# RWKV-7 triangular inverse: first three merge levels on TensorE replaced by an 8x8 solve on VectorE, in another written order

## The reference, cut to what matters

```
def step(S, inp):
    r_t, w_t, k_t, v_t, kk_t, a_t = inp
    sa = -jnp.einsum('bhvk,bhk->bhv', S, kk_t)
    S = (S * w_t[:, :, None, :] + sa[..., None] * (kk_t * a_t)[:, :, None, :]
         + v_t[..., None] * k_t[:, :, None, :])
    return S, jnp.einsum('bhvk,bhk->bhv', S, r_t)
```

## Time and profile before

| | us |
|---|---|
| time, median of 3 runs | 1287.76 (1287.63 to 1289.8) |
| the profiled execution: its own time | 1285.7 |
| the profiled execution: span of the trace | 1283.9 |
| busy in the span: PE / PEld / DVE / ACT / POOL | 1249.1 / 1005.3 / 625.1 / 407.1 / 498.9 |
| mean granted TensorE clock | 0.98 of full speed |

### The profile page before, as it was taken

The page is one execution under the profiler, slowest core; times in us unless marked ns, Lnnn a source line. Parts: engine busy times, 40 slices in busy tenths (PEclk is TensorE's granted clock), DMA queues, the critical chain, the costliest instruction groups (busy, mean ns, idle before and its releaser), DMA issues.

```text
span 1283.9 us, 21631 instructions
## 1 busy us (share of the span) xinstructions
PE 1249.1 (97%) x8772; PEld 1005.3 (78%) x8772; DVE 625.1 (49%) x954; ACT 407.1 (32%) x598; POOL 498.9 (39%) x368
## 2 busy tenths in 40 slices
PE   7999999999999999999999999989999999999996
PEld 5877778888888888877867777767788888888885
DVE  4624666441114434447557767776554311344333
ACT  4644433221112222244443435324322211222110
POOL 0541445454445555533122011103555544455541
PEclk9999999999999999999899988979999999999998
DMA  7211212222222222221011000100222222222211
GB/s 272 100 66 66 99 66 99 98 99 99 98 97 74 93 99 95 98 99 66 3 67 35 35 34 2 68 2 35 99 99 98 98 99 98 99 98 98 99 66 65
DMA packets 17783, 105.17 MB, mean 82 GB/s; under 512 B 1968, under 2 KB 2480, under 8 KB 6064
## 3 DMA queue, kind: packets, MB, share of 16 engines
q1 hardware_dynamic: 17280, 103.75, 23.2%
q10 hardware_dynamic: 432, 0.38, 0.1%
HBM read 102.03 MB, written 2.10 MB: 81 GB/s over the span
## 4 chain that ended last, share of the span: by engine, by line
PE 90%; issue 3%; DVE 3%; POOL 2%; ACT 1%; DMA 0%; DVEq 0%; SPq 0%; POOLq 0%; ACTq 0%
PE ps L1015 61%; PE ps L1109 7%; PE ps L1166 3%; PE ps L1143 2%; POOL w_lo L583 2%; PE ps L1078 2%; PE ps L1419 2%; PE ps L1397 2%; PE ps L1435 1%; PE ps L1342 1%; PE ps L1278 1%; DVE cv L2054 1%; PE ps L1455 0%; PE ps L1463 0%; PE ps L1522 0%
## 5 line engine op out<-in xcount | busy, mean ns | idle before, releaser
L583 POOL TENSOR_TENSOR w_lo<-w_raw,w_hi 128x512 fp32r<-128x512 f32 x360 | 493.2, 1400 | 752.9 <-ACT w_hi L676 266.6
L1015 PE MATMUL ps<-h_hi,w_hi 128*128 128x512 f32 x688 | 277.2, 403 | 0.1
L1015 PE MATMUL ps<-h_lo,w_hi 128*128 128x512 f32 x688 | 269.6, 392 | 0.0
L1015 PE MATMUL ps<-h_hi,w_lo 128*128 128x512 f32 x688 | 269.5, 392 | 0.0
L1015 PEld LDWEIGHTS ps<-h_hi,w_hi 128*128 128x128 f32 x688 | 130.1, 189 | 35.2 <-issue 7.4
L676 ACT ACTIVATE w_hi<-w_raw 128x2048 fp32r<-128x2048 f32 x50 | 95.7, 1913 | 194.7 <-PE ps L1015 143.4
L1015 PEld LDWEIGHTS ps<-h_hi,w_lo 128*128 128x128 f32 x688 | 130.1, 189 | 27.8
L1015 PEld LDWEIGHTS ps<-h_lo,w_hi 128*128 128x128 f32 x688 | 130.4, 190 | 25.7 <-issue 0.5
L1015 PE MATMUL ps<-f_hi,w_hi 128*128 128x512 f32 x384 | 149.4, 389 | 0.0
L1015 PE MATMUL ps<-f_lo,w_hi 128*128 128x512 f32 x384 | 149.4, 389 | 0.0
L1015 PE MATMUL ps<-f_hi,w_lo 128*128 128x512 f32 x384 | 149.4, 389 | 0.0
(11 more groups left out here) (319 smaller groups left out, 1778.1 us busy)
## 6 DMA issues: line engine op xcount, KB each, us to landing
w_raw<-in_weights SPq DMA_DIRECT2D x91, 1024.0 KB, 4.9
x<-in_xT SPq DMA_DIRECT2D x8, 256.0 KB, 5.7
w_raw<-in_weights SPq DMA_DIRECT2D x8, 256.0 KB, 6.3
outT<-x SPq DMA_DIRECT2D x8, 256.0 KB, 2.0
masks_f<-in_masks SPq DMA_DIRECT2D x1, 512.5 KB, 6.2
sgu_ln<-in_sgu_ln SPq DMA_DIRECT2D x1, 512.0 KB, 8.2
low_w<-in_low_w SPq DMA_DIRECT2D x1, 512.0 KB, 7.2
sgu_w<-in_sgu_w SPq DMA_DIRECT2D x1, 256.0 KB, 6.7
```

What stands on the lines that cost most here:

```text
L583: piece = pool.tensor_tensor(w_lo[:, j, at], w_raw[:, j, at], w_hi[:, j, at].bitcast(f32), SUB)
L1015: mm = pe.matmul(bank(gb(g) if isinstance(i, int) else g % 2), w, r, start=(k == 0 and m == 0), stop=(k == K - 1 and m == 2))
```

## The change

Levels 0, 1 and 2 of the inverse leave TensorE. The diagonal 8x8 blocks (16 per matrix, 8 matrices) are inverted on VectorE by back substitution, and TensorE starts at level 3 (B = 8).

- `scores(c, 4)` on PE now makes L in 32x32 pieces (64x32 weights, twice as many matmuls as before); on DVE four masked copies gather the 8x8 blocks into `LT8` (128 partitions x 8 matrices x 8 columns).
- `solve(c, j)`, j = 6 down to 1, is new on DVE: a partition shuffle of 64 columns, a product with a broadcast column of `LT8`, and a sum, each waiting for the one before.
- `x_of(c)` is new on DVE: a masked copy of 512 columns spreads the solved blocks into `xtc`, and a 32x32 block transpose of 512 columns gives `xc`.
- ACT writes one identity per c and not two.
- The steps of levels 1 and 2 (`tx`, `dx`, `dxt`) are gone from all three lists, and the masks of the three levels with them; the lists stand in another order throughout: the same remaining steps, differently interleaved.

```diff
+BASE = 8
+FIRST_LEVEL = 3
+MERGES = LEVELS - FIRST_LEVEL
+X_STEPS = 4 + 3 * (BASE - 2) + 2
...
@@ scores(c, 4) on TensorE
-                        for to in COLUMN_HALVES:
-                            mm = pe.matmul(ps[to, 3 + h2, 32 * n:32 * n + 32], AR[r, c % 2, n, 0, to],
-                                           bT[r, n * P + to.start:n * P + to.stop:2], start=True, stop=True)
+                        for q in range(0, P, 32):
+                            mm = pe.matmul(ps[q:q + 32, 3 + h2, 32 * n:32 * n + 32],
+                                           bT[r, n * P + q:n * P + q + 32], AR[r, c % 2, n, 0, q:q + 32],
+                                           start=True, stop=True)
...
@@ tx on TensorE
-                if lv == 1:
-                    pe.wait_ge(s("x_init"), 4 * c + 2)
+                n = lv - FIRST_LEVEL
+                if n == 0:
+                    pe.wait_ge(s("x_step"), X_STEPS * (c + 1))
+                    pe.wait_ge(s("score_done"), 8 * c + 8)
                     pe.wait_ge(s("ktok1_done"), c + 1)
...
@@ on VectorE
+                for k in range(4):
+                    if c or k:
+                        dve.wait_ge(s("x_step"), X_STEPS * c + k)
+                    dve.copy_predicated(y4(LT8[:, :, :].rearrange("p y n -> p (y n)"), BASE), y4(mask(f"block{k}", 0, 8 * BASE), BASE),
+                                        ps[:, 3:5, 0:P].rearrange("p h (t n) -> p t h n", n=32)[:, :, :, BASE * k:BASE * k + BASE])\
+                       .then_inc(s("x_step"), 1)
+
+            def solve(c, j):
+
+                at = X_STEPS * c + 4 + 3 * (BASE - 2 - j)
+                z = LT8 if j == BASE - 2 else Z8
+                flat = lambda t: t[:, :, :].rearrange("p y n -> p (y n)")
+                dve.wait_ge(s("x_step"), at)
+                dve.stream_shuffle(flat(R8), flat(z), [BASE * (p // BASE) + j for p in range(32)]).then_inc(s("x_step"), 1)
+                dve.wait_ge(s("x_step"), at + 1)
+                tt(T8[:, :, :], R8[:, :, :], LT8[:, :, j:j + 1].broadcast_to([P, 8, BASE]), MUL).then_inc(s("x_step"), 1)
+                dve.wait_ge(s("x_step"), at + 2)
+                tt(flat(Z8), flat(z), flat(T8), ADD).then_inc(s("x_step"), 1)
+
+            def x_of(c):
+
+                at = X_STEPS * (c + 1) - 2
+                dve.wait_ge(s("x_step"), at)
+                dve.wait_ge(s("x_id"), c + 1)
+                dve.copy_predicated(xtc[:, :, :].rearrange("p y (b n) -> p y b n", n=BASE),
+                                    mask("blocks").rearrange("p (y b n) -> p y b n", b=8, n=BASE),
+                                    Z8[:, :, :].rearrange("p y (b n) -> p y b n", b=1).broadcast_to([P, 8, 8, BASE]))\
+                   .then_inc(s("x_step"), 1)
+                dve.wait_ge(s("x_step"), at + 1)
+                dve.transpose(xc[:, :, :].rearrange("p y n -> p (y n)"), xtc[:, :, :].rearrange("p y n -> p (y n)"))\
+                   .then_inc(s("x_step"), 1)
```

The parts of the written order on which most depends are those between `scores(c, 4)` and the first `tx` of c. On TensorE after the change, for c = 0, 1, 2, 3:

```diff
+            ("scores", 0, 4), ("slice", 7, 7), ("slice", 6, 0), ("zw", 1), ("tok_tr", 0, 0), ("tok_tr", 0, 1), *run("slice", 6, 1, 7),
+            ("tok_tr", 0, 2), ("slice", 6, 7), ("slice", 1, 0), ("slice", 1, 1), ("za", 1), ("tx", 0, 3, 0),
...
+            ("scores", 1, 4), ("slice", 10, 5), ("zw", 2), ("tok_tr", 1, 0), ("slice", 10, 6), ("slice", 10, 7),
+            ("tok_tr", 1, 1), ("tok_tr", 1, 2), *run("slice", 9, 0, 3), ("za", 2), ("post", 0, 0), ("tx", 1, 3, 0),
...
+            ("scores", 2, 3), *run("slice", 13, 0, 8), ("slice", 12, 0), ("scores", 2, 4), ("zw", 3), ("tok_tr", 2, 0),
+            ("slice", 12, 1), ("slice", 12, 2), ("tok_tr", 2, 1), ("tok_tr", 2, 2), ("za", 3), ("post", 1, 0), ("tx", 2, 3, 0),
...
+            ("scores", 3, 4), *run("slice", 21, 4, 8), *run("tok_tr", 3, 0, 3), ("post", 2, 0), ("tx", 3, 3, 0),
```

and on VectorE:

```diff
+            ("scores", 0, 4), ("evac_b", 5), ("evac_a", 7), *run("tap", 0, 4, 12), ("evac_b", 7), ("solve", 0, 6),
+            ("solve", 0, 5), ("solve", 0, 4), ("scan", 1), ("solve", 0, 3), ("solve", 0, 2), ("solve", 0, 1), ("x_of", 0),
...
+            *run("scores", 1, 2, 5), *run("tap", 1, 3, 8), ("evac_a", 10), ("tap", 1, 8), ("solve", 1, 6), ("solve", 1, 5),
+            ("solve", 1, 4), *run("tap", 1, 9, 13), ("solve", 1, 3), ("solve", 1, 2), ("solve", 1, 1), ("x_of", 1),
...
+            ("scores", 2, 3), ("scores", 2, 4), ("evac_b", 11), *run("tap", 2, 9, 13), ("scan", 3), ("tap", 2, 13), ("solve", 2, 6),
+            ("solve", 2, 5), ("solve", 2, 4), ("evac_a", 13), ("solve", 2, 3), ("solve", 2, 2), ("tap", 2, 14), ("solve", 2, 1), ("x_of", 2),
...
+            ("scores", 3, 3), ("scores", 3, 4), ("evac_a", 21), *run("tap", 3, 0, 6), ("solve", 3, 6), ("solve", 3, 5),
+            ("solve", 3, 4), ("tap", 3, 6), ("tap", 3, 7), ("solve", 3, 3), ("tap", 3, 8), ("tap", 3, 9), ("solve", 3, 2),
+            ("post_v", 2, 0), ("solve", 3, 1), ("x_of", 3),
```

More of the change, by code:

```diff
@@ L381, in build @@
[L381 to L390, removed]
@@ L407, in build @@
[L407 to L411, removed]
@@ L438, in build @@
+            ("out", 0, 3), ("out", 1, 3), ("out", 0, 4), ("out", 1, 4), ("out", 0, 5), ("out", 1, 5), ("out", 0, 6),
+            ("out", 1, 6), ("out", 0, 7), ("out", 1, 7),
         ]
         DVE1 = [
[L441 to L443 removed]
@@ L444, in build @@
-            ("dyn", 0, "k2"), ("dyn", 0, "kt"), ("dyn", 0, "rt"), ("dyn", 0, "rk"), ("dec", 0), ("evac_b", 14),
-            ("bonus", 0), ("scores", 0, 0), ("evac_a", 15), ("scores", 0, 1), ("evac_a", 5), ("scores", 0, 2),
-            *run("tap", 0, 0, 3), ("scores", 0, 3), ("tap", 0, 3), ("scores", 0, 4), ("evac_a", 7),
-            *run("tap", 0, 4, 7), ("scan", 1), ("dx", 0, 1, 0), ("dx", 0, 1, 1), ("dxt", 0, 1),
-            *run("tap", 0, 7, 11), ("dx", 0, 2, 0), ("dx", 0, 2, 1), ("dxt", 0, 2), ("tap", 0, 11), ("tap", 0, 12),
@@ new lines, in build @@
+            ("tap", 0, 1), ("scores", 0, 1), ("scores", 0, 2), ("tap", 0, 2), ("scores", 0, 3), ("tap", 0, 3),
+            ("scores", 0, 4), ("evac_b", 5), ("evac_a", 7), *run("tap", 0, 4, 12), ("evac_b", 7), ("solve", 0, 6),
+            ("solve", 0, 5), ("solve", 0, 4), ("scan", 1), ("solve", 0, 3), ("solve", 0, 2), ("solve", 0, 1),
+            ("x_of", 0), ("dec", 0), ("dx", 0, 3, 0), ("dx", 0, 3, 1), ("dxt", 0, 3), ("dx", 0, 4, 0),
+            *run("tap", 0, 12, 15), ("dx", 0, 4, 1), ("dxt", 0, 4), ("evac_a", 6), *run("tap", 0, 15, 20),
@@ new lines, in build @@
+            ("dx", 0, 5, 0), ("dx", 0, 5, 1), ("dxt", 0, 5), ("ks_v", 1), ("dec", 1), ("evac_a", 1), ("kn_v", 1),
+            ("s", 0, 0), ("evac_b", 6), ("dyn", 1, "at"), ("dyn", 1, "ab"), ("dyn", 1, "bt"), ("dyn", 1, "k2"),
+            *run("tap", 0, 20, 23), ("dyn", 1, "kt"), ("dyn", 1, "rt"), ("s", 0, 1), ("dyn", 1, "rk"),
+            *run("tap", 0, 23, 28), ("s", 0, 2), ("tap", 0, 28), ("bonus", 1), ("evac_b", 1), ("evac_a", 16),
+            ("evac_b", 16), ("tap", 0, 29), ("tap", 0, 30), ("evac_a", 17), ("scores", 1, 0), ("tap", 1, 0),
@@ new lines, in build @@
+            ("scores", 1, 1), ("tap", 1, 1), ("evac_a", 8), ("tap", 1, 2), *run("scores", 1, 2, 5),
+            *run("tap", 1, 3, 8), ("evac_a", 10), ("tap", 1, 8), ("solve", 1, 6), ("solve", 1, 5), ("solve", 1, 4),
+            *run("tap", 1, 9, 13), ("solve", 1, 3), ("solve", 1, 2), ("solve", 1, 1), ("x_of", 1), ("evac_b", 8),
+            ("dx", 1, 3, 0), ("dx", 1, 3, 1), ("scan", 2), ("dxt", 1, 3), ("dx", 1, 4, 0), ("dx", 1, 4, 1),
+            ("dxt", 1, 4), ("post_v", 0, 0), ("tap", 1, 13), ("dx", 1, 5, 0), ("dx", 1, 5, 1), ("post_v", 0, 1),
@@ new lines, in build @@
+            ("scores", 2, 0), ("evac_b", 18), ("evac_a", 19), ("scores", 2, 1), ("scores", 2, 2),
+            *run("tap", 2, 0, 3), ("evac_a", 11), *run("tap", 2, 3, 9), ("scores", 2, 3), ("scores", 2, 4),
+            ("evac_b", 11), *run("tap", 2, 9, 13), ("scan", 3), ("tap", 2, 13), ("solve", 2, 6), ("solve", 2, 5),
+            ("solve", 2, 4), ("evac_a", 13), ("solve", 2, 3), ("solve", 2, 2), ("tap", 2, 14), ("solve", 2, 1),
+            ("x_of", 2), ("dx", 2, 3, 0), ("dx", 2, 3, 1), ("dxt", 2, 3), ("tap", 2, 15), ("tap", 2, 16),
@@ new lines, in build @@
+            ("dyn", 3, "rt"), ("dyn", 3, "rk"), ("tap", 2, 28), ("s", 2, 2), ("evac_b", 12), ("bonus", 3),
+            ("tap", 2, 29), ("tap", 2, 30), ("scores", 3, 0), ("evac_a", 20), ("scores", 3, 1), ("scores", 3, 2),
+            ("evac_b", 20), ("scores", 3, 3), ("scores", 3, 4), ("evac_a", 21), *run("tap", 3, 0, 6),
+            ("solve", 3, 6), ("solve", 3, 5), ("solve", 3, 4), ("tap", 3, 6), ("tap", 3, 7), ("solve", 3, 3),
+            ("tap", 3, 8), ("tap", 3, 9), ("solve", 3, 2), ("post_v", 2, 0), ("solve", 3, 1), ("x_of", 3),
```

263 lines of the change are left out of this document (127 added, 136 removed), and 58 rows, old and new, of tables (ACT1, PE1).

## The result

| | before | after |
|---|---|---|
| median of 4 runs each, same chip, us | 1288.2 (1287.63 to 1289.8) | 1311.26 (1309.46 to 1311.45) |
| profiled execution, us (span) | 1285.7 (1283.9) | 1311.45 (1309.4) |
| mean granted clock | 0.98 | 0.952 |

The ratio is 1.0174, 95% interval 1.0156 to 1.0192: slower by 23 us. The forecast was slower, at 1299, with a range of its own up to 1308; the move on the profiled execution is 25.75 us where the sum gave 10.8. The time of one kernel moves with its clock from execution to execution: in a set of 19 runs beside the experiments, one of them slow and left out, the kernel before took 1279.5 us at a mean granted clock of 0.984 and 1297.2 at 0.970, so one trace of a kernel is one draw of where its clock falls.

What follows compares the result with a forecast made beforehand. Bound by TensorE's own queue for c = 0 to 2, by VectorE's taps in the last window. Terms summed to +10.8 us on 1285.7, 1296.5; with 2.1 for the median 1298.6, said as 1299; own range 1291 to 1308, full range 1278 to 1313.

Steps and rivals of the forecast that it cites:

- the sum gave 10.8: Whole kernel: -22.5 - 0.9 + 1.2 + 22 + 5 + 6 = +10.8 us on the profiled execution's 1285.7.
- the working gave 6.3, 7.6, 8.4: First `tx`, c = 0 to 2: gaps of 6.9, 8.2, 9.0 us, less some 0.6 each of existing waits; +22 together.
- +0.4: `scores(c, 4)` on TensorE: twice as many L matmuls add 0.4 us per c, 1.2 over c = 0 to 2.
- the forecast's 5: Last window, c = 3: VectorE's longer chain makes the last tap and `conv_mean` come 5 us later.
- Rival (2): VectorE's solves: shuffles at 0.75 us each cost 2.6 us more per c, +10.4 in all, 1309; chance 0.13.
- (1): Mixing stage: low stretches of c = 0 and 2 vanish, c = 1 gets none; about 1278; chance 0.22.
- (3): Mixing stage: later TensorE waits of c = 0 and 2 shrink, c = 1 keeps its clock; 1288 to 1289; chance 0.12.
- The clock: Levels 3 to 6 of c = 1: a new half-clock stretch behind the gap, 0 to +7.5 us, taken as +6.
- its 22.5: TensorE, c = 0 to 2: us saved by removing levels 1 and 2, some groups counted at half clock.
- For c = 0 and 2 the low stretch stays about as it is: Levels of c = 0 and 2: existing half-clock stretches of 10 and 20.5 us do not lengthen.
- 7.66 busy of 8.0 us: Trace before, c = 0: TensorE waiting between small matmuls, read as preceding the clock's fall to 0.50 at 613.9 us.
- the 14 us of c = 1: Trace before, c = 1: 14 us read as dense small matmuls that kept clock 1.00.

Runs made afterwards that it cites:

- (2): The changed kernel with useless 128x128x512 matmuls (36, 27, 30, 45) before the first `tx` of c = 0 to 3: 1279.6 us, ratio 0.9914.
- (6): The changed kernel with VectorE's six solves and `x_of` right behind the scores (c = 0: behind two evacuations), the taps later: 1285.3 us, ratio 0.9965.
- 3: Two kernels: the kernel before in the changed kernel's order, 1309.0 us; the changed kernel's solve in the order of the kernel before, 1305.8 us.
- 5: The changed kernel without its 18 solve operations per c, `x_of` copying the unsolved blocks: 1287.4 us, ratio 0.9987.
- 7: The changed kernel with ScalarE's cut of chunk 51, which releases GpSimd's subtractions, moved behind `tx(0, 4, 1)`: 1307.7 us, ratio 1.0145.

## Why the prediction was right in sign and wrong in size

**Right.** TensorE's wait stands at the first `tx` of each c, ended by the transpose of `xc`: 9.45, 6.96, 7.79 us where the working gave 6.3, 7.6, 8.4, and 11.4 at c = 3 for "over 12". The idle time for c = 0 to 2 rose by 22.0, against 21.1. The solve takes 0.77 to 0.78 against 0.82, shuffle 0.22 against 0.32, `x_of` 1.44 against 1.5; the L matmuls take 0.69 us from start to start against 0.60, so +0.09 where +0.4 was taken. Level 3 of c = 3 has all it needs 17.8 us into its window instead of 13.7: 4.1 for the forecast's 5. Rival (2), the dear shuffle, gives the right time, near 1309, for a wrong reason. Rivals (1) and (3), the clock given back or the gaps absorbed, did not occur: besides the wait at `tx` the idle time of c = 0 and 2 fell by 0.7 and 1.2 us (0.9 of it in the sum already), where (3) had 4.

**Wrong: the term "The clock", "I take +6", for c = 1 alone.** The windows of c = 0 to 2 grew by 11.1 together, and slices written ahead of the first put its start 2.3 later (601.5, 603.8): 13.4 in all, as the starts of the last window say (822.8, 836.2). Eighteen groups of 1.05 went (18.9 at full clock), the L matmuls brought 0.3, the idle time 22.0; what is left, 13.4 + 18.9 - 0.3 - 22.0 = 10.0, is the clock. On that footing the forecast had 6 less the 3.6 by which its 22.5 exceeds 18.9: 2.4. Another 7.0 lies in the last window, behind its wait (57.7 us from there to the end of `out`, before 50.6), where it had nothing. That is 14.6 of the 15 us missing; the waits came 0.9 over their term, the L matmuls and c = 3 each 0.9 under, and 1.2 lies outside the stage. The sentences that failed: "For c = 0 and 2 the low stretch stays about as it is" (10 became 21 us, 20.5 became 31), and the silence on c = 3 (14 became 38). The stretch that it did foresee, at c = 1, came: 27 us.

**Why it failed.** The forecast asked at which c a new wait would throw the clock, and not how long the clock then stays down. All four falls lie inside the new waits. For c = 0 to 2 the clock came back only 2.5 to 5.1 us after the next run of slices had begun, and in the new order that run stands behind level 4 (c = 0) or the first products of level 6 (c = 1 and 2): it begins at 637.1, 722.8 and 802.2 us. So the rest of the wait and all levels up to there ran at half clock. Before, slices at 618.4, between the levels of c = 0, had the clock back at 624.0. At c = 3 only two or three large matmuls at a time stand among the levels, and the clock stayed down until these had ended (882.3); before, the levels of c = 3 ran at full clock and it fell near their end, at 849.2.

That the wait is what throws the clock in this kernel is shown for each c: with useless large matmuls in its place the levels of c = 0, 2 and 3 kept full clock (2), and with the wait removed by VectorE's order alone those of c = 0 and 1 did (6). Counted over the changed kernel and the ten kernels of the experiments, four c each: 23 times TensorE waited 1.4 us or more at the first `tx`; once the clock was already down, and 22 times it fell in that wait or within 2 us behind it. 21 times the wait there was 1.2 us or less; six times the clock fell all the same, 2.0 to 2.9 us into the levels, and 15 times it did not. With useless large matmuls in front it held 11 times of 12, without them 4 of 9. So a wait is not needed for a fall, and dense small matmuls can hold the clock for 12 us and can lose it in 2; what decides between these was not found.

The earlier trace rows was also misread. The 7.66 busy of 8.0 us at c = 0 is one wait of 0.34 us, ended at 606.75; four groups of the levels, `zw` and `za` ran densely behind it before the clock fell. At c = 2 the wait of 0.83 us ended 3.8 us before the fall. And the 14 us of c = 1 are not small matmuls alone: they begin with two slices and hold a third, and five in a row stand just ahead (the timeline under 3).

The Trainium skill, "TensorE: Matmul & The Clock Gate", "HAM oscillation", lays half speed to waits between bursts. The four falls inside the waits agree with it. The old levels in the new order do not: at c = 1 to 3 the clock fell with no wait over 0.6 us there, and 56.3 us are lost in that trace.

Shown: that the wait costs its length (experiments 5 to 7); that it throws the clock (2, 6); that the changed kernel's low stretches for c = 0 to 2 run from the wait to the next run of slices. Argued only: that slices between the levels would have ended them sooner, from where the clock came back in the traces; no run moves slices there. Open: why the clock falls without a wait in some places and not in others with the same rows; why the two halves of 3 do not add; and whether small fillers without a wait behind them would have held it.

## What to carry to other kernels

A step moved off the bound engine is worth its time only if what replaces it does not stand in front of that engine's in-order queue: put the replacing chain first on its own engine (26 us here) before weighing its operations. A wait of the bound engine can cost more than its length, where the clock falls in it: read the granted clock in the wait and behind it, up to where it comes back, and see what the new order has written there. Take a fall of the clock in one trace as one draw: the same rows kept 1.00 in one kernel here and fell to 0.50 in another.

## What the runs showed of the hardware

- A wait of TensorE of 1.4 us or more in front of the first group of level 3 came with half clock each time, 23 of 23; in 22 of them the clock fell in the wait or within 2 us behind it.
- Small matmuls (64x64 weights, 32 columns) back to back held full clock for 12 us in some places (the kernel with the solves first, c = 1; the old levels in the new order, c = 0) and not in others (TensorE busy 32.00 of 32.00 us at 0.52). A group x32 goes from 1.05 to 1.71 us, less than double.
- Useless 128x128x512 matmuls in the four gaps of 7 to 11 us took 32 us off the kernel.
- GpSimd's subtraction of 512 columns stretched 64-column VectorE products and sums from 0.23 to 0.92 to 1.30 us and a scan from 1.23 to 2.30; the shuffle of the same size stayed at 0.22.
- A shuffle of 128x64 took 222 ns, a 32x32 block transpose of 128x512 took 712.
